# Neighbourhood bias bands: 128 transfers from one padded table, or one transfer of bands laid out per partition

## The reference, cut to what matters

```python
row_off = r0 + jnp.arange(win_h) - r + NA_WIN_H - 1
bias = jnp.take(jnp.take(rpb, row_off, axis=1), col_off, axis=2)
bias = bias.transpose(0, 2, 1, 3).astype(jnp.float32)
s_loc = jnp.einsum('bqhd,bkwhd->bhqkw', qr, kb, preferred_element_type=jnp.float32) * scale + bias[None]
s_loc = jnp.where(col_mask[None, None, :, None, :], s_loc, NEG_INF_2)
s_ctx = jnp.einsum('bqhd,bchd->bhqc', qr, k_ctx, preferred_element_type=jnp.float32) * scale
s = jnp.concatenate([s_loc.reshape(B, H, GRID_W, n_loc), s_ctx], axis=-1)
```

## Time and profile before

| | |
|---|---|
| time, median of 3 runs | 4130.7 us (4128.36 to 4131.1) |
| profiled execution: time, span | 4134.67 us, 4132.9 us |
| mean granted TensorE clock | 0.969 of full speed |
| PE busy | 3922.2 us, 95% of the span |
| DVE, ACT, POOL busy | 1101.4, 654.0, 248.0 us |
| moved by DMA | 489.69 MB, mean 118 GB/s |
| chain that ended last, by engine | PE 91%, DVE 3%, DMA 3%, ACT 1%, POOL 1%, issue 1% |

### The profile page before, as it was taken

One profiled execution on the slowest core, in us unless ns is written; L12 is line 12 of the kernel. 1 busy time (PEld: TensorE's weight loads), 2 busy tenths in 40 slices (PEclk: granted clock), 3 DMA queues, 4 the chain that ended last, 5 costly groups with the idle time before them and its releaser, 6 DMA issues.

```text
span 4132.9 us, 60701 instructions
## 1 busy us (share of the span) xinstructions
PE 3922.2 (95%) x27010; PEld 2668.3 (65%) x27010; DVE 1101.4 (27%) x2366; ACT 654.0 (16%) x1509; POOL 248.0 (6%) x390
## 2 busy tenths in 40 slices
PE   5999999899999999969999999999999988999998
PEld 3446745554445666758748677666666667888887
DVE  1100143751002322212200531445554454000001
ACT  1100022420002122102100310222222222000000
POOL 0000000000000000240000000211111211000000
PEclk9999999999999999989999999999999986999999
DMA  8443323224333433496421134211111110544443
GB/s 337 176 153 122 123 92 112 82 84 180 144 132 122 156 130 123 163 183 255 163 82 64 59 123 133 66 40 44 44 44 34 34 33 5 168 152 153 152 157 122
DMA packets 77444, 489.69 MB, mean 118 GB/s; under 512 B 10480, under 2 KB 14576, under 8 KB 23552
## 3 DMA queue, kind: packets, MB, share of 16 engines
q1 hardware_dynamic: 70560, 462.45, 32.2%
q0 software_dynamic: 6624, 23.35, 2.3%
HBM read 481.57 MB, written 4.19 MB: 118 GB/s over the span
## 4 chain that ended last, share of the span: by engine, by line
PE 91%; DVE 3%; DMA 3%; ACT 1%; POOL 1%; issue 1%; DVEq 0%; ACTq 0%; POOLq 0%
PE ps L955 50%; PE ps L1055 9%; PE ps L949 7%; PE ps L1220 4%; PE ps L894 3%; PE ps L1015 3%; PE ps L1034 2%; PE ps L1205 2%; PE ps L952 2%; DMA w<-in_wi 2%; PE ps L1025 1%; POOL zone L832 1%; PE ps L902 1%; PE ps L1291 1%; PE ps L1124 1%
## 5 line engine op out<-in xcount | busy, mean ns | idle before, releaser
L955 PE MATMUL ps<-h,w 128*128 128x256 f32 (+1 forms) x4992 | 1554.9, 464 | 54.8 <-DMA w<-in_wi 37.3
L955 PEld LDWEIGHTS ps<-h,w 128*128 128x128 f32 x4992 | 943.5, 194 | 510.4 <-issue 412.7
L955 PE MATMUL ps<-y,w 128*128 128x256 f32 (+1 forms) x1792 | 507.9, 442 | 0.0
L955 PEld LDWEIGHTS ps<-y,w 128*128 128x128 f32 x1792 | 338.9, 190 | 153.9 <-issue 121.7
L1055 PE MATMUL ps<-h,w 128*128 128x256 f32 (+1 forms) x1024 | 413.2, 521 | 1.3 <-issue 1.3
L949 PE MATMUL ps<-w,h 128*128 128x256 f32 x1280 | 278.7, 380 | 0.0
L949 PEld LDWEIGHTS ps<-w,h 128*128 128x128 f32 x1280 | 243.6, 190 | 38.0 <-issue 6.1
L1055 PEld LDWEIGHTS ps<-h,w 128*128 128x128 f32 x1024 | 176.7, 194 | 91.4 <-issue 69.1
L1220 PEld LDWEIGHTS ps<-zone 64*64 64x64 f32 x4608 | 153.3, 139 | 47.6 <-issue 32.8
L832 POOL TENSOR_TENSOR zone<-zone 128x256 f32<-128x256 f32 x160 | 133.9, 851 | 796.1 <-ACT zone L1653 604.9
L894 PE MATMUL ps<-w,zone 128*32 128x256 f32 x2304 | 149.8, 403 | 29.6 <-DVE zone L2216 11.5
(11 more groups left out here) (306 smaller groups left out, 3109.0 us busy)
## 6 DMA issues: line engine op xcount, KB each, us to landing
w<-in_wm SPq DMA_DIRECT2D x144, 1024.0 KB, 8.0
w<-in_we SPq DMA_DIRECT2D x52, 1024.0 KB, 5.0
w<-in_w SPq DMA_DIRECT2D x48, 1024.0 KB, 5.1
w<-in_wmg SPq DMA_DIRECT2D x48, 1024.0 KB, 5.1
w<-in_wi SPq DMA_DIRECT2D x34, 1024.0 KB, 5.1
w<-in_wo SPq DMA_DIRECT2D x32, 1024.0 KB, 5.0
w<-in_wrw SPq DMA_DIRECT2D x32, 1024.0 KB, 5.1
w<-in_wbr SPq DMA_DIRECT2D x48, 512.0 KB, 4.4
```

Of the source, the lines that this page charges most:

```text
L955: last = mm(pass_psum(s, q), rows[:, n * P:(n + 1) * P], src[k], start=(k == 0), stop=(k == s.kt - 1))
```

## The change

The DRAM input `rpb` is built on the host as 128 bands, one for each partition, of 6 x 16 x 64 values (3.1 MB in place of 0.12 MB), and is loaded by one transfer. The count on which DVE waits falls from 130 to 3 completions (window mask, bias, column mask). The values in SBUF are the same.

```diff
@@ lay_out
-    a["rpb"] = rpb
+    a["rpb"] = np.stack([rpb[5 - half:11 - half, :, 63 - c:127 - c] for half in range(2) for c in range(GRID)])
@@ gpsimd
             pool.dma_start(xc[:, :, :], A["ctx2"]).then_inc(s_x2, 16)
-            for half in range(2):
-                for c in range(GRID):
-                    pool.dma_start(rpb[half * GRID + c:half * GRID + c + 1, :, :, :].rearrange("p a b c -> p (a b) c"),
-                                   A["rpb"][5 - half:11 - half, :, 63 - c:127 - c].rearrange("a b c -> (a b) c")
-                                   .rearrange("(o a) c -> o a c", o=1)).then_inc(s_bias, 16)
+            pool.dma_start(rpb, A["rpb"]).then_inc(s_bias, 16)
             pool.wait_ge(s_mrows, 72)
@@ vector
-            dve.wait_ge(s_bias, 16 * (2 + 2 * GRID))
+            dve.wait_ge(s_bias, 16 * 3)
```

## The result

The changed kernel took 4094.99 us (median of 4 executions, 4094.81 to 4097.69) beside 4130.9 of the kernel before (4 executions): ratio 0.9917, with a 95% interval of 0.9898 to 0.9936. In a second comparison it took 4093.49 beside 4137.59, ratio 0.9895 (0.9880 to 0.9910). It is faster, by 0.8 to 1.1%. The forecast was 4086.0 us, 44.7 us less than before; the first comparison gave 35.9 us, the second 44.1.

What follows compares the result with a forecast made beforehand. PE bounds the kernel but waits for weights delayed by 128 small bias transfers around 1737 to 1855 us. Loss of 52.2 less 7.5 remaining gives 44.7 us; 4130.7 - 44.7 = 4086.0 us, range 4079 to 4095.

Steps and rivals of the forecast that it cites:

- The loss in the stretch before: First gate1 panel (1737.56) to wo1 (1855.14): PE's weight waits and slower clock cost 52.2 us.
- what stays: Loss left in the stretch after the change: 5.1 us first wait plus 2.4 for the clock, 7.5 us.
- the later gaps: PE's weight waits after the first in the stretch: vanish, as weights alone need 257 GB/s of 422.
- DVE's and POOL's parts: POOL's 127 saved issues (64.55 us) and DVE's wait on fewer completions: worth nothing by themselves.
- the first wait: PE's wait near 1741 us for the first weight half: 5.1 us in place of 9.0.
- rows in turn: Engines alternate rows of POOL's and SP's queues, so bias and low mod half land together at 1756.3.
- The upper bound of the gain: If the first weight half landed undisturbed, in 5.1 us, nothing is lost: gain 52.2 us (4078.5), 6 in 100.
- from the stretch to the median: Takes the stretch's 44.7 us off span, profiled time and the median 4130.7 alike, giving 4086.0 us.
- POOL's queue served first: Rival: x_context and bias go ahead of the weight half; gap 12.4 us, gain 37.4, 4093.3 us; 8 in 100.
- bytes and not the form of the transfers: Rival: weights suffer from the bias's bytes, which are the same, so nothing changes: 4130.7 us; 3 in 100.
- The slower rival: Bias still moves at 48 GB/s, unpaced; low mod half lands at 1814, 12 us slower, 4142.7 us; 3 in 100.
- The lower rate of 352 GB/s: Rival: full engines in the stretch keep to 352 GB/s; loss 11.3 us, gain 40.9, 4089.8 us; 5 in 100.

Runs made afterwards that it cites:

- The experiment with 4 KB rows and the late bias: Changed kernel with the bias loaded 190 us later and x_context reloaded in four transfers of 4 KB rows: 4085.51 us, ratio 0.9894.
- the one without the late bias: Changed kernel with x_context reloaded in four transfers of 4 KB rows, bias load at its old place: 4095.56 us, ratio 0.9910.
- the late bias: Changed kernel with the single bias transfer moved behind POOL's wait for the last mod panel, 190 us later: 4090.50 us, ratio 0.9906.
- whole rows: Changed kernel's table loaded by 128 transfers of one partition each, contiguous 24 KB rows, in rising order: 4120.24 us, ratio 0.9972.
- other order and small pieces: Kernel before, with its own table and 256-byte pieces, its 128 transfers reordered to partitions 37 apart: 4114.62 us, ratio 0.9953.
- whole rows in the other order: Changed kernel's table loaded by 128 one-partition transfers of whole rows, each 37 partitions further on: 4103.75 us, ratio 0.9920.
- the columns: Changed kernel's bias load cut into 96 transfers, each of 256 bytes in all 128 partitions: 4095.52 us, ratio 0.9897.
- the kernel with small pieces: Changed kernel, still one transfer into 128 partitions, but a 256-byte hole behind every 256 bytes of the source: 4099.41 us, ratio 0.9926.
- the run with both cuts: Late bias and x_context in 4 KB rows, with x_context cut likewise at the end of attention b: 4083.36 us, ratio 0.9880.

## Why the prediction was right, and where it was wrong

**Right: the place and the kind of the loss, and its size with some luck.** The loss in the stretch before was put at 52.2 us, what stays at 7.5, the gain at 44.7. By three profiles of before (mean 121.3 us) and two of the changed kernel (mean 75.9) the stretch is 45.4 us shorter. The mod panel does not wait, the later gaps are gone but for the 1.49 us of the second profile, and DVE's and POOL's parts are worth nothing. The window from 1740 to 1756 us shows 401 GB/s, just above the 400 asked for. The two terms were each too small: measured in the prediction's way, with 65.3 us of work in the stretch, the loss before is 54.0 us in the mean of three and what stays is 8.7 in the mean of two. The errors nearly cancel. Nor was the first wait cut from 9.0 us: it was 9.00, 4.44 and 4.46 us in the three profiles of before and 6.71 and 4.51 in the two of the changed kernel. The gain is made in the four waits behind it.

**Right: rows in turn.** The forecast let the bias land together with the low mod half, 20.7 us after the trigger. They landed together, 21.4 us after 1739.19 and 20.9 after 1739.90, so at 1760.6 and 1760.8, 22 us after the trigger. The experiment with 4 KB rows and the late bias confirms the rule by its number (7.18 us for 7.0); the one without the late bias does so in kind, with a second wait larger than expected. The two other profiles with 4 KB rows have 7.50 and 7.92 us for this half. The rule does not cover the small pieces: cut short, they should have let the weights through earlier, and PE waited longer.

**Off: the first wait.** "both land near 1746.4, 10.6 us after the issue" was taken from one execution of another place. Here the half took 12.15 us in the first profile, 11.8 with the late bias and 9.95 in the second profile of the changed kernel. The wait of 5.1 us became 6.7 and 4.5. The stretch of the first pair gave 42.9 us, not 44.7, and 1.6 of these 1.8 us are this term. The upper bound of the gain, 52.2 us if the first half came early, is in doubt as well: with 4 KB rows for x_context alone the half landed after 7.50 us and the first wait was 2.06, and yet the stretch took 77.2 us, since the next half was late.

**The step that failed: from the stretch to the median.** The prediction said that the profiled execution's span and time "both should fall by 44.7", and then "The median before is 4.0 us below that execution's time, so the median after is 4130.7 - 44.7". It gave no reason why what lies ahead of the stretch should repeat, nor why the changed kernel's median should lie as far below its own profiled execution. Neither did. The trigger came 3.07 us late, and the changed kernel's median (4094.99) lies 0.18 us above its profiled execution (4094.81), where that of before lies 3.77 below (4130.9 and 4134.67). The sum for the first comparison is 44.7 - 1.76 in the stretch - 3.07 ahead of it - 3.95 from execution to median = 35.9 us, which is what was measured (4130.9 - 4094.99). The last term was not seen in a trace. So 8.8 us of the forecast were missing, 7.0 of them by this step. The measured 4094.99 lies 5 us outside the 4083 to 4090 that had 75 in 100, and it is luck that it still falls within 4079 to 4095: that range was drawn from the one unknown wait and left no room for the scatter of a kernel whose 35 executions ran from 4124.4 to 4144.3 us. The 44.1 us of the second comparison, close to the forecast, are chance in the same way.

Of the 3.1 us ahead of the stretch, 2.0 are at the end of attention b, where the changed kernel's PE timeline has a wait of 2.07 us and a slow half pass behind it, where rows 7 has 1.74 and none:

```profile
949.22 8.83 PE L951 MATMUL ps<-h,w 128*128 128x512 f32 x16 [2.07 <-DMA w<-in_we]
```

Whether that is all chance is open. In the four profiles of kernels with the old table this wait was 1.62 to 1.86 us and no half pass behind it was slow. In the nine with a new table and the same code there it was 1.70 to 2.27, with a slow half pass in five. The mean trigger of the nine is 1734.8 us and of the four 1734.1, so the difference is below 1 us, if it is one.

**What stays open.** Over the executions of the table the medians are 4133.4 (35) and 4094.9 (8), 38.5 us apart, and the profiled stretches 45.4. The gain in the stretch does reach the time of the executions that were profiled: their means are 4136.5 and 4092.2 us, 44.2 apart. But the three of before, at 4134.7, 4136.6 and 4138.1, all lie above the median of the 35, and the two of the changed kernel, at 4094.8 and 4089.7, at or below that of the 8. So part of the difference can be that the stretches profiled before are longer than most; no profile of a short one was had. The kernels with 128 transfers into single partitions scattered by 20 us (before), 16 (whole rows) and 20 (other order and small pieces), and the others, whole rows in the other order among them, by 3 to 8. But the first three are ranges of 35, 10 and 8 executions and most of the others of 4, so it is only likely, and not shown, that much of the scatter is made in the stretch. The recurrence stage behind, between the load of the chunk masks and the reload of x_latent, took 1012.4 to 1024.8 us over the profiles, whichever kernel, and adds to it.

**The rivals.** POOL's queue served first had 4093.3 us, nearer to the measured median than the forecast, but not by its mechanism: it asked for a first wait of 12.4 us, and 6.7 and 4.5 were seen. The late bias excludes it too: without a bias in the queue the first wait was the same. That bytes and not the form of the transfers hold the weights up is excluded by the columns, with the same bytes. The slower rival, a bias that keeps its old rate, did not occur, though its premise was half true: the destination was the larger part of the old cost, and the change removed it. The two causes that the prediction left undecided as "changes nothing in the sum" are now told apart: in the stretch, the new table's whole rows are worth 17 us with single partitions in order (121.3 to 104.2) and 9 in the other order (94.9 to 85.8), and the single-partition destination 28 (104.2 to 75.9); of these, the order of the partitions alone makes 18 (104.2 to 85.8). What in the old table costs the 17 us is not separated: its pieces are short, they begin at offsets that shift by 4 bytes from partition to partition, and they come again and again from the same 0.12 MB. The experiment with small pieces has only the first of these, in one transfer, and cost 8 to 9 us. The lower rate of 352 GB/s is not seen either: from 1742 to 1758 us the changed kernel moved

```profile
1742.00:1758.00 16.00, 9.29 (x34) 7.55 (x34) 0.40 (x1) 0.82 (x2) 0.00 (x0) 0.79 1.01 428
```

428 GB/s, where the Trainium skill has about 358 on the page that the prediction names, "DMA: Bandwidth & Descriptors", section Bandwidth. The measurement decides.

## What to carry to other kernels

A transfer that nobody waits for can be the dearest one if it shares the engines with a stream that is due. Look for a full DMA share with few bytes moved, and then at the destination first: spread each transfer over all partitions, or, where it must go into one, do not send neighbours one after another. Where a background load in large rows meets a stream of weights, its row length against the weights' decides who gets through: cut its rows or issue it later, and look at everything in the queue, or the wait only moves to the next weight half. Pieces as short as 256 bytes cost again. And before a gain found in one profiled execution is subtracted from a median, look how far the kernel's executions lie apart, and make the range at least as wide.

## What the runs showed of the hardware that was not expected

- A transfer of 24 KB into one partition, sent to neighbouring partitions in a row, landed after 16.4 us in the median; the same transfers 37 partitions apart after 8.0.
- 256-byte source pieces in one 3 MB transfer cost 8 us of the stretch (84.7 us against 76.5 and 75.3), and in 96 transfers of one such piece per partition about 1 (77.6).
- A wait of PE of 1.74 us left the work behind it at full clock (3.72 us for a half pass), one of 2.06 did not (5.41 us). The length of the wait alone does not decide it: at the end of attention b a half pass of 7.13 us at full clock was slow (8.83) behind a wait of 1.93 us in the kernel with small pieces, and not slow (7.13) behind 1.97 us in the second profile of the changed kernel. So the expectation of the run with both cuts, that the clock had fallen wherever the wait was 1.9 us or more, misread one profile.
